# One block for the gate stage and the expert stage of a PEER decoder block, coefficients two tiles behind u, last one-hots on VectorE

## The reference

```python
def expert_block(args):
    hb, ib, gb = args
    u = jnp.take(u_tab, ib, axis=0)
    act = jax.nn.gelu(jnp.einsum('btd,bted->bte', hb, u), approximate=False)
    vv = jnp.take(v_tab, ib, axis=0)
    return jnp.einsum('bte,bted->btd', gb * act, vv)
```

## Time and profile before

| | |
|---|---|
| median of 3 runs | 1856.44 us (1854.17 to 1859.69) |
| the profiled execution, its span | 1856.8 us, 0.36 us above that median |
| TensorE (PE) busy | 1768.2 us, 95% of the span |
| VectorE (DVE), ScalarE (ACT), GpSimd (POOL) busy | 1307.3, 742.8 and 764.5 us |
| gate stage, expert stage | 971.8 to 1224.9 us, 1224.9 us to the end |
| DMA | 432.64 MB, mean 233 GB/s over the span |

### The profile page before, as it was taken

One profiled execution on the slowest core, in us unless ns is written; L12 is line 12 of the kernel. 1 busy time (PEld: TensorE's weight loads), 2 busy tenths in 40 slices (PEclk: granted clock), 3 DMA queues, 4 the chain that ended last, 5 costly groups with the idle time before them and its releaser, 6 DMA issues. The chain is left out here.

```text
span 1856.8 us, 31058 instructions
## 1 busy us (share of the span) xinstructions
PE 1768.2 (95%) x11485; PEld 1564.7 (84%) x11485; DVE 1307.3 (70%) x2777; ACT 742.8 (40%) x1227; POOL 764.5 (41%) x449
## 2 busy tenths in 40 slices
PE   3999999999998989999999999879999999999998
PEld 2666888878877889999999999879998888888887
DVE  5993454553224679878869999756787888777777
ACT  4332332242234233333337767633333333333334
POOL 2333232344442448777753333122454443332330
PEclk9998999999999999999999999989999999999999
DMA  9661101022322249888868999978899999889883
GB/s 356 217 233 71 36 16 34 25 91 91 102 79 103 91 141 314 282 292 292 286 235 281 341 311 331 319 264 285 287 317 337 370 370 359 326 320 328 316 325 145
DMA packets 179267, 432.64 MB, mean 233 GB/s; under 512 B 15816, under 2 KB 91720, under 8 KB 179040
## 3 DMA queue, kind: packets, MB, share of 16 engines
q1 hardware_dynamic: 125088, 273.71, 42.5%
q0 software_dynamic: 36864, 134.23, 20.3%
q10 hardware_dynamic: 17216, 23.36, 3.4%
HBM read 383.54 MB, written 47.71 MB: 232 GB/s over the span
## 5 line engine op out<-in xcount | busy, mean ns | idle before, releaser
L201 POOL DMA_INDIRECT own_rows<-in_peer_v_dram,own_row x128 | 212.3, 1659 | 330.8 <-DVE y_own L2094 312.7
L1988 PE MATMUL banks<-v_hi,coef_lo 128*128 128x512 f32 x756 | 294.6, 390 | 0.0
L1988 PE MATMUL banks<-v_lo,coef_hi 128*128 128x512 f32 x756 | 294.5, 390 | 0.0
L1988 PE MATMUL banks<-v_hi,coef_hi 128*128 128x512 f32 x756 | 294.1, 389 | 0.1
L201 POOL DMA_INDIRECT own_rows<-in_u_rows_dram,own_row x128 | 160.6, 1255 | 233.1 <-DVE own_rows L1733 178.8
L2079 DVE TENSOR_TENSOR v_lo<-weight_ring,v_hi 128x1024 fp32r<-128x1024 f32 x128 | 156.5, 1222 | 24.7 <-ACT v_hi L2027 22.7
L1988 PEld LDWEIGHTS banks<-v_hi,coef_hi 128*128 128x128 f32 x756 | 142.0, 188 | 29.5 <-issue 0.5
L1988 PEld LDWEIGHTS banks<-v_hi,coef_lo 128*128 128x128 f32 x756 | 141.9, 188 | 29.5
L1988 PEld LDWEIGHTS banks<-v_lo,coef_hi 128*128 128x128 f32 x756 | 141.9, 188 | 28.9
L2094 DVE SCALAR_TENSOR_TENSOR y_own<-own_rows,own_coef,y_own 128x1024 f32<-128x1024 f32 x128 | 163.8, 1279 | 1.9 <-DVE y_own L2094 0.5
L1397 PE MATMUL banks<-h_hi,wring_hi 128*128 128x384 f32 (+2 forms) x448 | 155.2, 347 | 4.0 <-ACT gelu_early L1479 2.9
(11 more groups left out here) (393 smaller groups left out, 4346.1 us busy)
## 6 DMA issues: line engine op xcount, KB each, us to landing
weight_ring<-in_peer_v_dram SPq DMA_DIRECT2D x128, 512.0 KB, 5.4
weight_ring<-in_peer_u_dram SPq DMA_DIRECT2D x68, 512.0 KB, 4.5
ada<-in_w_ada_dram SPq DMA_DIRECT2D x48, 512.0 KB, 5.7
gate_scratch<-gate_block SPq DMA_DIRECT2D x48, 512.0 KB, 7.0
gate_tiles<-gate_scratch SPq DMA_DIRECT2D x32, 768.0 KB, 6.9
gelu_scratch<-gelu_early ACTq DMA_DIRECT2D x104, 192.0 KB
gelu<-gelu_scratch SPq DMA_DIRECT2D x104, 192.0 KB, 5.6
u_early<-in_peer_u_dram SPq DMA_DIRECT2D x36, 512.0 KB, 7.1
```

The costliest lines, as they stand in the source:

```text
L201: pool.indirect_dma_start(own_rows[:, n % R], None, tables[n // NS], bass.IndirectOffsetOnAxis(ap=own_row[:, n % NS:n % NS + 1], axis=0)). ...
L1988: last = nc.tensor.matmul(y_bank(t, half)[:], w[:, j, t * P:(t + 1) * P], x[:, j, c], start=(first and n == 0), stop=False)
```

## The change

It does four things.

1. The two stages share one block (all semaphores are made ahead of it), so there is no barrier between them. TensorE waits for the copy of unit 6, SP for the stores of gates and GELUs, and the buffers of the expert stage are placed in another order in memory.
2. The last iteration of the gate stage has its u tiles where the others have them, behind units 5 and 6, and VectorE makes `hot2` of its unit 7.
3. In the expert stage ScalarE and VectorE handle coefficients and v tile of position m - 2 in the step in which the u tile of m is handled, and TensorE makes y of position m - 3 behind u of m, instead of m - 1.
4. The loads of u tiles 2 and 3 of the expert stage stand behind the last stores of the gate stage in SP's queue, ahead of the wait for those stores. The memset of `y_own` moves to position 0.

The core of the diff (lines whose indentation alone changes are left out; `...` marks what is cut):

```diff
@@ program
-                scatter_stage(nc, a, env, spill, acts)
-            expert_stage(nc, a, env, spill, acts, out)
+                scatter_sems(env)
+                block = late.enter_context(nc.Block())
+                scatter_stage(nc, a, env, spill, acts, block)
+            expert_stage(nc, a, env, spill, acts, out, block)
@@ scatter_stage
-        tiles = {False: {u: (m,) for m, u in enumerate(U_UNITS)},
-                 True: {**{u: (m,) for m, u in enumerate(U_UNITS[:-2])}, NU - 1: (U_ITER - 2, U_ITER - 1)}}
+        tiles = {u: (m,) for m, u in enumerate(U_UNITS)}
...
+        def act_makes(u, final):
+            return u in by_act and not (final and u == NU - 1)
@@ scatter_stage, vector
-                    if u not in by_act:
+                if not act_makes(u, final):
...
-                            unit(i, u + 1)
+                        unit(i, u + 1, final and u + 1 == NU - 1)
@@ scatter_stage, tensor
-                        if u in by_act:
+                    if act_makes(u, final):
...
                 body(NR - 1, True)
+            pe.wait_ge(*A.after(f"unit{NU - 2}", NR - 1))
@@ scatter_stage, scalar
-                        if u + 2 in by_act:
+                    if act_makes(u + 2, not more):
                             one_hot(i, u + 2)
...
                     body(i, i < NR - 1)
-                for s in s_gel:
-                    act.wait_ge(s, G0 + 16 * (NR * U_ITER // 2))
@@ scatter_stage, sync
                     store(NR * SLOTS - 1, 1, q)
+            for m in range(2, 4):
+                sp.wait_ge(u_lo_ready, m - 1)
+                sp.dma_start(ut[:, m % 2], a["peer_u"][N_EARLY + m]).then_inc(s_u[m % 2], 16)
                 for s in stored:
                     sp.wait_ge(s, 16 * NQ * (NR + 1))
+            for s in s_gel:
+                sp.wait_ge(s, G0 + 16 * (NR * U_ITER // 2))
@@ expert_stage
+        LAG = 2
@@ expert_stage, sync
-                    if p < NL and p >= 2:
+                if 4 <= p < NL:
@@ expert_stage, tensor
-                u_products(0, 0)
-                for j in range(1, G):
+            for j in range(G):
                     u_products(j, j % 2)
-                        y_products(j - 1, j - 1, first=(j == 1))
+                if j > LAG:
+                    y_products(j - LAG - 1, j - LAG - 1, first=(j == LAG + 1))
                 with pe.Fori(1, GL) as i:
                     for j in range(G):
                         u_products(i * G + j, j % 2)
-                        y_products(i * G + (j - 1), (j - 1) % G)
+                    y_products(i * G + (j - LAG - 1), (j - LAG - 1) % G)
...
@@ expert_stage, scalar
-                for p in range(NX):
+            for m in range(NX + LAG):
+                p = m - LAG
...
+                if m < NL:
+                    act.wait_ge(u_done, m + 1)
+                    nc.scalar.activation(gel[:, m % G, :], bank[m % 2][:, 0:TD], ACT.Gelu).then_inc(gelu_ready, 1)
+                if m + 2 < NL:
+                    split_u(m + 2)
+                if p >= 0:
                     split_c(p)
                     if p + 1 < NX:
                         split_v(p + 1)
@@ expert_stage, vector
-                nc.vector.memset(y_own[:], 0.0).then_inc(own_zero, 1)
                 n = U_DONE
-                for p in range(NX):
+            for m in range(NX + LAG):
+                p = m - LAG
+                if m + 1 < NL:
+                    split_u(m + 1)
+                if p < 0:
+                    continue
...
+                if p == 0:
+                    nc.vector.memset(y_own[:], 0.0).then_inc(own_zero, 1)
```

More of the change, by code:

```diff
@@ L209, in program @@
             env["u_hi_ready"], env["u_lo_ready"] = sem(late, "x_u_hi"), sem(late, "x_u_lo")
+            env["late"] = late
             with ExitStack() as pick:
@@ L1939, in expert_stage @@
         TOKS = (ND, *range(ND))
[L1940 removed]
+        half_done, scaled = g_["x_half_done"], g_["x_scaled"]
+        LAG = 2
         def y_bank(t, half):
             return bank[2 + 2 * t + half]
[L1945 to L2006 removed]
@@ new lines, in _, with u_products, y_products @@
+        @block.gpsimd
+        def _(pool):
+            for n in range(U_DONE + R, 2 * NS):
+                fetch(pool, n)
+        @block.tensor
+        def _(pe):
+            def u_products(m, b):
+                pe.wait_ge(u_lo_ready, m + 1)
+                if not (isinstance(m, int) and m < 2):
+                    pe.wait_ge(gelu_ready, m - 1)
+                for k in range(KT):
+                    for n, (w, x) in enumerate(((u_hi, h_hi), (u_hi, h_lo), (u_lo, h_hi))):
+                        last = nc.tensor.matmul(bank[b][:, 0:TD], w[:, b, k, :], x[:, k, 0:TD], start=(k == 0 and n == 0), stop=(k == KT - 1 and n == 2))
+                last.then_inc(u_done, 1)
+            def y_products(e, j, first=False):
+                pe.wait_ge(v_lo_ready, e + 1)
+                pe.wait_ge(c_lo_ready, e + 1)
```

628 lines of the change are left out of this document (305 added, 323 removed).

## The result

The changed kernel takes 1862.33 us (median of 19 runs, 1860.13 to 1866.40) where the kernel before takes 1858.50 us beside it on the same chips (19 runs, 1854.17 to 1864.41). The ratio is 1.003, with a 95% interval of 1.0022 to 1.0037: slower by 0.3%. Forecast were 1847.8 us and a gain; the result is slower, and outside the range. The profiled execution has a span of 1861.6 us against 1856.8.

A forecast was written before the change was run, and what follows sets the result against it. TensorE, busy 95% of the span, was taken as the bound. 20.9 - 0.6 - 6.9 - 1.8 - 3.0 = 8.6 us gained, a median of 1847.8 us; range 1841.4 to 1853.

The forecast's parts named there:

- The prize: At the seam between gate and expert stage, 20.9 us is all the change can save; other TensorE work stays the same.
- The gain is taken back elsewhere: Rival: something unseen at the seam takes the gain back, about 1856 us; chance 0.04.
- Slower: Rival: from position 24 on VectorE, waiting for row fetches, sets the pace; 1866 us; chance 0.05.
- Part 2: Last gate iteration: moved tiles cover the copy of unit 5; VectorE's added one-hots priced at nothing, 3.2 us if uncovered.
- Wait before u tile 1: Start of the expert stage: u tile 1's halves come late, at 1210.7 against 1210.06, a loss of 0.6 us.
- The hole before u tile 2: Expert stage start: TensorE waits 6.9 us for a load behind the gate stores; ends 3.3 and 10.9 us.
- the end of 3.3: Short end of the hole before u tile 2: load lands 4.4 us after issue, hole 3.3 us.
- The clock: After the hole before u tile 2 the granted clock falls once, costing 1.8 us.
- The coefficient in time for y 0: First y product: gate matrix lands by 1224, coefficient's low half ready near 1230.5, 1.5 us to spare; priced at nothing.
- The switch: Where the u tiles end: the lag makes TensorE wait for VectorE's `coef_lo`, 3.0 us, between 2 and 4.5.

The follow-up runs named there:

- the kernel with `y_sq` last: The changed kernel with the small buffer `y_sq` allocated last, as in the kernel before, instead of ahead of `coef`: 1850.53 us, ratio 0.9969 to the kernel before.
- the last experiment: Changed kernel with `y_sq` last, early u tile 2 load, moved own rows; now u tile 3's load behind the second of the last four stores: 1846.92 us.

## Why the prediction was wrong

**The step that failed** is the end of "The prize": "the rest of PE's work is the same in amount". It is the same in number of matmuls, but not in time. The order of buffers, which the change's first item names, got no price at all and no reason for having none; it costs 14.4 us. The rival "The gain is taken back elsewhere" had 0.04 and looked for it at the seam, at 1856; "Slower" had 0.05 and looked for it in VectorE. Neither saw this: VectorE ended no wait of TensorE behind the switch. It is shown by three kernels: the placement alone makes the kernel before as slow as worked out (13.7 us), the placement alone taken back makes the changed one faster (11.8 us by the medians, 13.4 by the traces from unit 5: 14.4 less the 0.9 that the switch then costs more), and a move of all operands together does nothing. As what would make it wrong the prediction named loads, VectorE and waits of TensorE; it had no line for a matmul that takes longer without a wait. The trace of before could give it no price, but the code shows that distances between operands change, and the prediction could have named that as a risk.

**The rest of the sum**, by its own terms:
- Part 2 was priced at nothing beside its gain, and that holds: no idle before unit 7.
- Wait before u tile 1: 0.6 forecast; 1208.43 - (1190.26 + 17.9) = 0.3 measured.
- The hole before u tile 2: 6.9 forecast, from the end of u tile 1 to the start of u tile 2. In the same terms it measured 1221.05 - 1208.43 - 4.18 = 8.4 (8.16 by the trace's idle time). Two sizes were off and partly cancelled. The load was issued 1212.60 - 1190.26 = 22.3 us behind unit 5, where the forecast had 1211.3 - 1192.16 = 19.1: the four stores took 7.3 us from the copy, not 3.97. The loads of tiles 2 and 3 landed 5.7 to 6.1 us after their issue (the source view of L1913), where I had 8.0. The mechanism was right; it stood in a ring behind the stores. The Trainium skill's rule (page DMA: Bandwidth & Descriptors, section Queues, rings and completion order), by which the hole is 5.7 us at least, agrees with 8.4; the end of 3.3, which it excluded, did not come.
- The clock: 1.8 forecast, 10.92 - 8.36 = 2.6 measured. The low clock ran into u tile 3 as well. (Where the prediction calls 6.9 us longer than both holes, it compares with the 2.4 and 5.3 us after which the clock fell; the hole of 11.81 us was longer.)
- The coefficient in time for y 0: priced at nothing, with 1.5 us to spare. No wait is seen, and 1.5 us were to spare (its low half ended at 1229.89 + 0.56 = 1230.45, y 0 started at 1231.97). That is room only because TensorE is late itself: in the last experiment, where it comes earlier, this is a hole of 6.07 us.
- The switch: 3.0 forecast, on top of what before lost there. From start to start it measured 2.5 - 0.4 = 2.1 us in the changed kernel and 3.4 - 0.4 = 3.0 with the short pitch, which the forecast reckoned with. The place (positions 23 and 24 of y) and the cause (VectorE behind its own rows) were right, the cause as shown by moving three rows. That the size fits to 0.1 us is luck in part, as 1.2 us of the forecast were a guess.

So without the term of the pace the sum is 20.9 - 0.3 - 8.3 - 2.6 - 3.0 = 6.7 us, with the numbers of the kernel with `y_sq` last (its hole is 1223.56 - 1211.05 - 4.18 = 8.3). That kernel gained 6.7 by its trace and 7.7 by its medians, at 1850.53 us. The forecast of 8.6 is near for that kernel, and too high by the hole and its clock.

What stays open: why a remainder of 64 costs 6.7 ns a matmul and one of 128 5.8. That weight loads and the stream of the moving operand meet in the same part of memory is only a guess, from the fact that a distance counts and the place doesn't.

## What to carry to other kernels

- When a change reorders buffers, work out the distance from weights to moving operand before and after, and count matmuls in 100 us of a stretch that is 100% busy at a clock of 1.00. Here a 64-byte buffer in between cost 14 us of 1860, and a trace that looks for waits shows nothing of it.
- A load that must be early stands in the queue ahead of big stores, but each step forward pushes what is behind: look at the next thing wanted, and stop where the hole moves to a later consumer (u tile 2, then 3, then the coefficient, which waited behind the split of u tile 4).
- A barrier ends with the last of several engines. Taking work from in front of one of them may only change which one that is (GpSimd's drain before, the wait for the gate stores with the moved tiles alone).
- A lag pays at the start of a stage and costs where its other work ends; the work of a helper engine can be moved away from that place (three rows, 2.6 us).

## What the runs showed of the hardware

- The pitch of these fp32r 128x512 matmuls at a clock of 1.00 was 226.7 ns where the distance between weights and moving operand was a multiple of 512 bytes, 232.4 ns at a remainder of 128 and 233.3 at one of 64 (443, 432 and 430 or 431 matmuls in a stretch of 100 us). I had not expected a dependence on placement. The Trainium skill, page TensorE: Matmul & The Clock Gate, section Step-by-step: what each phase is for, says that the two operands have independent read ports and that weight loads take no bandwidth from the running matmul; by it, I would expect the placement to change nothing, and the measurement decides against that for these fp32r matmuls. Whether it is the weight loads that take the time no run here shows.
- GpSimd's drain at the end of the gate stage lasted 8.96 us before and 10.27 us with the moved tiles alone. It ended 6.8 us (1224.66 against 1217.82) and 8.2 us (1212.67 against 1204.51) behind the end of the last row fetch's instruction, within the 4.3 to 9.9 us that such fetches took to land; that it waits for them is read from that.
- The clock fell about 4 us after the work ended at the seam (u tile 1 ended near 1212.6, the stretch 1216 to 1217 has 0.64), between the 2.4 and 5.3 us seen before, and it came back to 1.00 only behind 1227, 6 us after the work began at 1221.05.
